# Sums of squares from the turned inputs, the order of two steps in the cross output, and where the mid tiles lie

## The reference, cut to what matters

```python
def rms_norm(x, g):
    y = x * lax.rsqrt(jnp.mean(x * x, axis=-1, keepdims=True) + RMS_EPS)
    return y * g

xn = rms_norm(h, norm_mix); proj = xn @ w_in               # h = x
# A: chunked attention, B: RWKV-7 time mixing, C: sliding-window attention, all read proj
h = h + concat([y_a, y_b, y_c]) @ w_out
xn = rms_norm(h, norm_x); mn = rms_norm(mem, norm_mem)      # cross attention, 4 heads of 128
q, k, v = xn @ x_wq, mn @ x_wk, mn @ x_wv
h = h + softmax(q k^T * 128**-0.5) v @ x_wo
h = h + relu(rms_norm(h, norm_mlp) @ mlp_w1)**2 @ mlp_w2   # width 8192
out = rms_norm(h, norm_final)
```

## Time and profile before

| | |
|---|---|
| median of 3 runs | 2789.34 us (2787.43 to 2789.41) |
| profiled execution, its own time | 2788.95 us |
| span of that execution, first to last instruction | 2787.2 us |
| TensorE matmul busy | 2723.8 us, 98% |
| VectorE busy | 1224.2 us, 44% |
| ScalarE busy | 803.2 us, 29% |
| GpSimd busy | 127.5 us, 5% |
| mean granted TensorE clock | 0.993 |
| DMA | 255.52 MB, mean 92 GB/s |

### The profile page before, as it was taken

How to read it: one execution, slowest core, us unless ns; L and a number is a source line. 1 busy time by engine, 2 the same in 40 slices (tenths; PEclk the granted TensorE clock), 3 DMA queues, 4 the chain that set the end, 5 groups by cost and what they waited for, 6 DMA issues and landing times.

```text
span 2787.2 us, 44304 instructions
## 1 busy us (share of the span) xinstructions
PE 2723.8 (98%) x18352; PEld 2158.9 (77%) x18352; DVE 1224.2 (44%) x1884; ACT 803.2 (29%) x1315; POOL 127.5 (5%) x240
## 2 busy tenths in 40 slices
PE   8999999999998999998899999999999999999997
PEld 6877777777777766886688888888888888888885
DVE  5266666666435545334433333333333333333333
ACT  4222222222124444344332221222212222122232
POOL 3000111001121110000000000000000000000000
PEclk9999999999999999999999999999999999999998
DMA  5321111111236522221133323322332223223322
GB/s 217 121 60 47 48 47 52 44 53 47 63 117 217 170 70 67 85 89 53 61 99 98 95 95 98 98 93 95 98 98 94 94 98 98 92 96 98 98 92 111
DMA packets 73148, 255.52 MB, mean 92 GB/s; under 512 B 8928, under 2 KB 9056, under 8 KB 71088
## 3 DMA queue, kind: packets, MB, share of 16 engines
q1 hardware_dynamic: 65664, 226.78, 25.4%
q0 software_dynamic: 7344, 26.69, 2.8%
HBM read 243.22 MB, written 10.22 MB: 91 GB/s over the span
## 4 chain that ended last, share of the span: by engine, by line
PE 95%; DVE 2%; DMA 1%; ACT 1%; issue 1%; DVEq 0%; POOL 0%; ACTq 0%; POOLq 0%
PE ps L1125 28%; PE ps L1126 26%; PE ps L1127 26%; PE ps L1144 9%; PE ps L1356 1%; PE ps L1335 1%; PE ps L1344 1%; DMA h<-in_mem_turned 1%; PE ps L1138 1%; DVE h L996 0%; DVE w_lo L710 0%; PE ps L1201 0%; PE ps L1198 0%; PE ps L1192 0%; PE ps L1181 0%
## 5 line engine op out<-in xcount | busy, mean ns | idle before, releaser
L710 DVE TENSOR_TENSOR w_lo<-w_raw,w_hi 128x1024 fp32r<-128x1024 f32 (+2 forms) x440 | 505.2, 1148 | 1163.0 <-ACT w_hi L434 1163.0
L434 ACT ACTIVATE w_hi<-w_raw 128x1024 fp32r<-128x1024 f32 (+2 forms) x440 | 438.9, 998 | 1566.0 <-PE ps L1127 1562.2
L1125 PE MATMUL ps<-act_hi,w_hi 128*128 128x512 f32 x1792 | 731.8, 408 | 14.9 <-DVE w_lo L710 11.5
L1127 PE MATMUL ps<-act_hi,w_lo 128*128 128x512 f32 x1792 | 701.6, 392 | 0.0
L1126 PE MATMUL ps<-act_lo,w_hi 128*128 128x512 f32 x1792 | 700.6, 391 | 0.0
L1125 PE MATMUL ps<-w_hi,mid_hi 128*128 128x512 f32 x1088 | 429.4, 395 | 8.1 <-DVE act_lo L752 6.7
L1126 PE MATMUL ps<-w_lo,mid_hi 128*128 128x512 f32 x1088 | 430.2, 395 | 0.0
L1127 PE MATMUL ps<-w_hi,mid_lo 128*128 128x512 f32 x1088 | 424.1, 390 | 0.0
L1125 PEld LDWEIGHTS ps<-act_hi,w_hi 128*128 128x128 f32 x1792 | 337.3, 188 | 108.0 <-DVE w_lo L710 12.0
L1127 PEld LDWEIGHTS ps<-act_hi,w_lo 128*128 128x128 f32 x1792 | 337.3, 188 | 73.0
L1126 PEld LDWEIGHTS ps<-act_lo,w_hi 128*128 128x128 f32 x1792 | 337.7, 188 | 68.7 <-issue 5.8
(11 more groups left out here) (273 smaller groups left out, 2404.7 us busy)
## 6 DMA issues: line engine op xcount, KB each, us to landing
w_raw<-in_w_rest SPq DMA_DIRECT2D x320, 512.0 KB, 3.4
w_raw<-in_w_pairs SPq DMA_DIRECT2D x112, 384.0 KB, 3.1
x_t<-in_x_turned SPq DMA_DIRECT2D x8, 512.0 KB, 8.7
x_mix<-in_x SPq DMA_DIRECT2D x4, 1024.0 KB, 13.3
qk<-scr_qkv POOLq DMA_DIRECT2D x16, 256.0 KB, 3.7
h<-in_x POOLq DMA_DIRECT2D x4, 1024.0 KB, 11.4
out<-h SPq DMA_DIRECT2D x4, 1024.0 KB, 4.3
scr_qkv<-pad POOLq DMA_DIRECT2D x15, 256.0 KB, 3.8
```

Of the source, the lines that this page charges most:

```text
L434: return nc.scalar.activation(dst, src, ACT.Copy, scale=scale)
L710: V.tensor_tensor(dst, w_raw[:, slot, 0:dst.shape[-1]], high.bitcast(F32), ALU.subtract).then_inc(s["w_split"], 1)
L1125: mm(dst, a_hi, b_hi, start=start, stop=False)
L1127: return mm(dst, a_lo, b_hi, start=False, stop=stop)
```

## The change

Five things are done.

1. x and mem are no longer loaded untransposed. ScalarE squares each turned tile (`squared`, into four buffers), VectorE adds the 16 squares up (`summed`), and one float32 ones matmul over the sum (`row_of_sums`) gives the sum of squares of every token on all partitions. Mean (`row_mean`, VectorE), root (`row_root`, ScalarE) and reciprocal (`inverse_row`, VectorE) are then done on the whole row, 512 or 256 wide. For x the squares stand in units 0 to 5 of g = 0, four tiles in each of units 0 and 1 and two in each of units 2 to 5. The matmul stands at p = 18, the start of unit 6. For mem they stand with the gained tiles at p = 13 to 20, and the matmul at p = 21 as before.
2. The values of the memory are scaled by the row where they leave PSUM, as the keys are; the later copy to `xv_tok` has no scale.
3. At the start the gain vector is loaded by SP as its first DMA. ScalarE and VectorE take tile 0, then the first weight unit, then tile 1; TensorE begins when tile 0 is there, and does all three outputs of tile 0 first.
4. In the cross output `turned_lo` stands ahead of `add_set`.
5. `rmem` goes and `rq` grows from 32 to 128 bytes, so everything behind it moves by 64 bytes: `h`, `mid_hi`, `mid_lo` and the RWKV tiles begin at 128 modulo 512.

```diff
-        rmem = sb("rmem", [P, 2])
-        rq = sb("rq", [P, 2, TT])
+        rq = sb("rq", [P, 8, TT])
...
-        x_mix = s1("x_mix", [P, TT, D])
+        x_sq = s1("x_sq", [P, 4, SEQ])
+        x_sum = s1("x_sum", [P, SEQ])
...
-        memx = h[:, 0:2, :]
+        mem_sq = h[:, 0, 0:4 * N_MEM].rearrange("p (i n) -> p i n", n=N_MEM)
+        mem_sum = h[:, 0, 4 * N_MEM:5 * N_MEM]
...  SP
+            sp.dma_start(gain[:, :, :], gains).then_inc(s["gain_in"], 16)
             for u in range(RAW):
                 turned_pair(u)
...
-                sp.dma_start(x_mix[:, u - RAW, :], x[(u - RAW) * P:(u - RAW + 1) * P, :]).then_inc(x_in[u - RAW], 16)
...  GpSimd
-            pool.dma_start(gain[:, :, :], gains).then_inc(s["gain_in"], 16)
+            step(nc.gpsimd.memset(ones[:, :], 1.0))
+            pool.sem_inc(s["ones_set"], 1)
...
-                    for t in range(2):
-                        pool.dma_start(memx[:, t, :], mem[t * P:(t + 1) * P, :]).then_inc(s["mem_in"], 16)
...  ScalarE
+            def squared(j, kt, dst, src):
+                if kt >= 4:
+                    act.wait_ge(s["sum_ready"], KT * j + kt - 3)
+                nc.scalar.activation(dst[:, kt % 4, :], src[:, kt, :], ACT.Square).then_inc(s["sq_ready"], 1)
+
+            def row_root(j, row, b, n):
+                act.wait_ge(s["row_mean"], j + 1)
+                nc.scalar.activation(row, row, ACT.Sqrt).then_inc(s["row_root"], 1)
...
                 if g == G_IN - 1 and p == 8:
-                    act.wait_ge(s["mem_in"], 32)
-                    for t in range(2):
-                        square_sum(t, 0, memx[:, t, 0:D // 2], mid_hi[:, 0:2, :].rearrange("p a b -> p (a b)"))
-                    root(1, 2)
                     act.wait_ge(s["memt_in"], 16)
                 for kt in mem_tiles(p, g):
+                    squared(1, kt, mem_sq, mem_t)
                     gained_hi(kt, 2, mem_hi, mem_t)
                 if g == G_IN - 1 and p == 23:
-                    act.wait_ge(s["row_mm"], 2)
-                    copy(mem_row, ps[:, 3, 0:N_MEM]).then_inc(s["row_ready"], 1)
+                    row_root(1, mem_row, 3, N_MEM)
...
-                    if g == 0 and u in (5, 6):
-                        for t in (2 * u - 10, 2 * u - 9):
-                            act.wait_ge(x_in[t], 16)
-                            square_sum(t, 0, x_mix[:, t, 0:D // 2], ps[:, 6:8, :].rearrange("p a b -> p (a b)"))
-                    if g == 0 and u == UNITS - 1:
-                        root(0, TT)
-                        act.wait_ge(s["consts"], 1)
-                        act.wait_ge(s["row_mm"], 1)
-                        copy(rms_row[:, :], bank(3)).then_inc(s["row_ready"], 1)
+                    if g == 0 and u < 6:
+                        for kt in (range(4 * u, 4 * u + 4) if u < 2 else range(2 * u + 4, 2 * u + 6)):
+                            squared(0, kt, x_sq, x_t)
+                    if g == 0 and u == 6:
+                        row_root(0, rms_row[:, :], 3, SEQ)
...
-                copy(xv_tok[:, kb, :], bank(6), scale=rmem[:, kb:kb + 1]).then_inc(s["xvt_ev"], 1)
+                copy(xv_tok[:, kb, :], bank(6)).then_inc(s["xvt_ev"], 1)
...  VectorE
+            def summed(j, kt, total, sq):
+                dve.wait_ge(s["sq_ready"], KT * j + kt + 1)
+                if kt == 0:
+                    V.tensor_copy(total, sq[:, 0, :]).then_inc(s["sum_ready"], 1)
+                else:
+                    dve.wait_ge(s["sum_ready"], KT * j + kt)
+                    V.tensor_tensor(total, total, sq[:, kt % 4, :], ALU.add).then_inc(s["sum_ready"], 1)
+
+            def row_mean(j, row, b, n):
+                dve.wait_ge(s["row_mm"], j + 1)
+                V.tensor_scalar(row, ps[:, b, 0:n], 1.0 / D, RMS_EPS, ALU.mult, ALU.add).then_inc(s["row_mean"], 1)
+
+            def inverse_row(j, row):
+                dve.wait_ge(s["row_root"], j + 1)
+                V.reciprocal(row, row).then_inc(s["row_ready"], 1)
...
                 for kt in mem_tiles(p, g):
+                    summed(1, kt, mem_sum, mem_sq)
                     gained_lo(1, kt, 2, mem_hi, mem_lo, mem_t)
+                if g == G_IN - 1 and p == 22:
+                    row_mean(1, mem_row, 3, N_MEM)
+                if g == G_IN - 1 and p == 23:
+                    inverse_row(1, mem_row)
...  VectorE, cross output
                 lo_next(G_XO, u)
+                if u % 2 and u > 1:
+                    turned_lo(3, u // 2 - 1, 3, tiles_of(act_hi), tiles_of(act_lo))
                 if u % 2:
                     add_set(UNITS * G_XO + u + 1, (S_XO + u // 2) % 2, u // 2)
-                if u % 2 and u > 1:
-                    turned_lo(3, u // 2 - 1, 3, tiles_of(act_hi), tiles_of(act_lo))
...  TensorE
+            def row_of_sums(j, total, n):
+                pe.wait_ge(s["ones_set"], 1)
+                pe.wait_ge(s["sum_ready"], KT * (j + 1))
+                mm(ps[:, 3, 0:n], ones[:, :], total, start=True, stop=True).then_inc(s["row_mm"], 1)
...
-                if g == 0 and p == 22:
-                    pe.wait_ge(s["diag_ready"], TT)
-                    row_of_roots(TT)
+                if g == 0 and p == 18:
+                    row_of_sums(0, x_sum[:, :], SEQ)
                 if g == G_IN - 1 and p == 21:
-                    pe.wait_ge(s["diag_ready"], TT + 2)
                     pe.wait_ge(s["var_eps"], PAIRS)
-                    row_of_roots(2)
+                    row_of_sums(1, mem_sum, N_MEM)
...
-                        pe.wait_ge(s["norm_lo"], 2 * u + 2)
+                        pe.wait_ge(s["norm_lo"], 2 * u + 2 if u else 1)
```

More of the change, by code:

```diff
@@ L484, in _ @@
             act.wait_ge(s["gain_in"], 16)
-            for n in range(SPL_IN - 1):
+            act.wait_ge(xt_in[0], 16)
+            gained_hi(0, 0, act_hi, x_t)
+            hi_in(0)
+            gained_hi(1, 0, act_hi, x_t)
+            for n in range(1, SPL_IN - 1):
                 x_hi(n)
@@ L756, in _ @@
             dve.wait_ge(s["zeroed"], 1)
-            for n in range(SPL_IN - 1):
+            dve.wait_ge(xt_in[0], 16)
+            gained_lo(0, 0, 0, act_hi, act_lo, x_t)
+            lo_in(0)
+            gained_lo(0, 1, 0, act_hi, act_lo, x_t)
+            for n in range(1, SPL_IN - 1):
                 x_lo(n)
@@ L911, in _ @@
                         lo_in(n)
[L912 to L918 removed]
+                    if g == 0 and u < 6:
+                        for kt in (range(4 * u, 4 * u + 4) if u < 2 else range(2 * u + 4, 2 * u + 6)):
+                            summed(0, kt, x_sum[:, :], x_sq)
+                    if g == 0 and u == 6:
+                        row_mean(0, rms_row[:, :], 3, SEQ)
+                        inverse_row(0, rms_row[:, :])
                     if g == 1 and u == 0:
                         dve.wait_ge(s["in_evac"], 3)
+                        dve.wait_ge(s["consts"], 1)
                         dve.wait_ge(s["lmu_in"], 16)
@@ L1003, in add_scaled_set, with scaled_by_row @@
                                            ALU.mult, ALU.add).then_inc(s["bank_evac"], 1)
+            def scaled_by_row(units, dst):
+                dve.wait_ge(s["w_used"], units)
+                dve.wait_ge(s["row_ready"], 2)
+                for m in range(4):
+                    V.tensor_tensor(dst[:, m, :], ps[:, m, 0:N_MEM], mem_row, ALU.mult).then_inc(s["bank_evac"], 1)
             def copy_set(units, sidx, dst, n):
@@ L1127, in split_mm @@
                 return mm(dst, a_lo, b_hi, start=False, stop=stop)
-            def row_of_roots(tiles):
-                pe.wait_ge(s["consts"], 1)
-                for t in range(tiles):
-                    last = mm(ps[:, 3, t * P:(t + 1) * P], ones[:, :], diag[:, t, :], start=True, stop=True)
-                last.then_inc(s["row_mm"], 1)
+            def row_of_sums(j, total, n):
+                pe.wait_ge(s["ones_set"], 1)
+                pe.wait_ge(s["sum_ready"], KT * (j + 1))
+                mm(ps[:, 3, 0:n], ones[:, :], total, start=True, stop=True).then_inc(s["row_mm"], 1)
             def turn_h(k, kt):
@@ L1303, in _ @@
                             kt = 2 * u + k
+                            if g == 0 and kt == 1:
+                                pe.wait_ge(s["norm_lo"], 2)
                             if kt == 0 and g:
```

49 lines of the change are left out of this document (12 added, 37 removed).

## The result

The changed kernel takes 2773.15 us (median of 4 runs, 2771.8 to 2775.31) beside 2789.38 us for the kernel before (4 runs, 2787.43 to 2791.83): ratio 0.9942, 95% interval [0.9925, 0.9959]. It is 16.2 us faster where 28 us were forecast, and 2773.15 lies outside the range of 2757 to 2769. The profiled execution took 2775.31 us, 2.2 above its median, so that its span is only 13.6 us shorter than that of before.

A forecast was written before the change was run, and what follows sets the result against it. TensorE, busy 2723.8 of 2787.2 us, was taken as the bound, leaving idle time and time per matmul. Terms -4.5 + 0.6 - 0.2 - 16.2 - 7.3 = -27.6 us on 2788.95 gave 2761.3 us, range 2757 to 2769.

The forecast's parts named there:

- the small products: Unit 7 of g = 0: eight small float32 matmuls, 2.08 us at the lower clock, replaced by one ones matmul of 1.0.
- Start and g = 0: Start to g = 1: TensorE starts at 7.35, waits 1.1 us for the sum in unit 6; -4.5 us, bounds -2.5 and -5.6.
- Mem row: g = 14: the 2.57 us wait goes, TensorE waits 2.9 for mem's sum; +0.6 us, bounds -0.5 and +3.5.
- the bound not taken: Mem row's upper bound: +3.5 us, with 0.42 us squares and adds and one more lower-clock stretch of 1.7.
- Cross output: Low halves ahead of the adds: three waits go, 10.5 us, and the slow stretches behind them, 5.7; -16.2 us.
- Where mid lies: Mid's tile from 64 to 128 modulo 512: 7.0 us as stationary operand, 0.3 moving; -7.3 us, bounds 0 and 7.6.
- the rival of another reason: Mid is slower for its role or how far up it lies, not its address: 2768.6 us; chance 0.13.
- The rule of the Trainium skill that the prediction weighed: Back-to-back 512-column matmuls 215.7 ns apart, no address term; by it mid's move is worth nothing, time 2768.6 us.
- VectorE being late in g = 0 and g = 14: Waits for the sums grow by 1.8 and 1.3 us, with 1.7 each of lower clock: 2767.8 us; chance 0.14.
- The cross output's wait staying: Cross output: the wait stays for something behind the same semaphore: 2777.5 us; chance 0.03.
- the small matmuls paying for the move: RWKV part: some 7,500 small matmuls each lose 6.6 ns by the 64-byte move, 50 us: 2811 us; chance 0.03.
- The rival on the slower side: The slower rival: RWKV's small matmuls pay for the 64-byte move, 2811 us; chance 0.03.

The follow-up runs named there:

- run 1: Changed kernel with 64 semaphore increments that nobody waits for at the start of TensorE's program: 2765.13 us, ratio 0.9908.
- run 5: Changed kernel with 8 increments at the start of TensorE's program: 2781.32 us in one run.
- run 9: Kernel before with one TensorE instruction fewer, a second wait for the same constants ahead of the row of mem: 2813.74 us, ratio 1.0099.
- run 2: Kernel before with 210 increments at the start of TensorE's program, which did not fit there: 2816.14 us, ratio 1.0085.
- run 3: Kernel before with one edit alone, the cross output's low halves ahead of the addition: 2772.99 us, ratio 0.9937.
- run 4: Changed kernel with the old layout, mid at 64 modulo 512 and all later tiles 64 bytes lower: 2778.97 us, ratio 0.9956.
- run 12: Changed kernel with the old order of the cross output and the old layout: 2797.09 us, ratio 1.0024.
- run 6: Changed kernel with 24 increments, mem's product at p = 23, and mem's views at 64 modulo 512 with mid at 128: 2761.32 us, ratio 0.9898.
- run 7: As run 6, but mid at 256 and the mem views at 192 modulo 512: 2779.32 us in one run.
- run 8: As run 6, but mid at 320 and the mem views at 256 modulo 512: 2767.57 us in one run.
- run 10: Changed kernel with 24 increments, mem's product at p = 23, weights and mid at 256 modulo 512, act at 128: 2787.53 us in one run.
- Run 11: As run 6, with 448 bytes behind mid so that the tiles behind it are at 64 modulo 512 again: 2761.40 us, ratio 0.9897.

## Why the prediction failed

**The step that failed is one that it does not have.** The sum has no term for where TensorE's loop lies among the blocks of its program. It costed the small products by their time alone (2.08 us for the eight of x), and put the 16 instructions that go, eight matmuls and eight weight loads, at nothing as instructions ahead of a loop. With 16 fewer the loop's body reaches over eight blocks instead of seven: 1598 instructions are six blocks and 62, so they fit into seven if the loop begins among the first 195 instructions of a block, and it went from the first back to the 241st. Here seven blocks stayed loaded through the turns (109 blocks in all), and with eight, nine were brought each time (163). The holes behind that cost 10.5 us in the trace of the changed kernel. That is 10.5 of the 13.9 us between the forecast's -27.6 and the measured -13.7; the mem row has 1.5 and the mem groups 1.3 of the rest. Runs 1, 5 and 9 moved the loop by increments or by one wait alone, and the holes went, moved and came. Run 1, where they are gone, has 2765.13 us, which lies in the range of the forecast; the 10.5 taken off 2773.15 would make 2762.6, against 2761 forecast. That all 10.5 come back in the medians is not shown: 8.0 did.

Why the hole's length changes is worked out, not measured. Hole and matmuls ahead of it make about the same sum: 2.5 to 3.1 us with none, 2.4 to 2.9 with three (0.7 us), 2.4 to 3.0 with six (1.4 us). With the end 46 instructions behind, some 20 matmuls or 4.6 us lie ahead (an estimate by 227 ns each), more than that sum, and no hole is listed.

The Trainium skill has the sizes, in "Runtime: NRT & Kernel Launch", section "Instruction fetch mechanics": TensorE's instruction memory holds 128 KiB and is refilled in blocks of 16 KiB, which are 256 instructions. An estimate from these figures is room for eight blocks, so that a loop over seven fits beside one fetched ahead and a loop over eight does not; the traces agree (0 and 9 blocks a turn). The same section of the Trainium skill also says that this memory is only two cache lines, and that a taken branch to a block outside the current window of two waits for its fetch. By that a loop over seven blocks would be fetched again in each turn; here none of it was, and the branch took 0.21 us, so for TensorE the measurement decides against it. It also says that crossing a block is mostly hidden. That agrees with run 2, whose window of w1 groups has 87.11 us against 87.04, and not with a block's end 1 to 16 instructions behind the turn, where the holes are 0.9 to 3.1 us.

**Start and g = 0**: right in mechanism, -4.1 for -4.5. The first matmul came at 7.81 and not 7.35, since tile 0 was begun at 5.38 and not 4.9 (the terms of the forecast add up to 7.26, not 7.35). From there to unit 6 TensorE took 27.4 us against 27.0 before, mostly because the lower clock at the start lasted 4.7 us of it and not 4.1. So unit 6 was reached at 35.2 and not 34.3. The sum was done at 35.7, later than the 35.4 forecast. The wait is 0.66 and not 1.1 only because TensorE came late to it, and the clock stayed at 1.00 behind it.

**Mem row**: the wait of 2.9 came as 3.18, and g = 15 follows unit 7's end by 2.94 where the forecast has 3.1. What was wrong is the bound not taken: behind the wait the granted clock was at its lower level from 855.58 to 858.99, so unit 7 ended 1.7 us later. The forecast had named that 1.7 as the upper bound, and +2.1 is inside its bounds. The clock did not fall each time: behind the same wait it fell in runs 4, 5 and 12 (3.0 to 3.4 us of waiting) and not in run 1 (2.92 us). The wait's length alone does not decide it: at g = 15 it fell in the kernel before at a wait of 2.67 us and stayed in run 4 at one of 2.93. Run 6 shows that the wait was avoidable: two places later the product finds its sum done, 3.9 us earlier at g = 15.

**Cross output**: right in mechanism and size. -16.6 over its stretch, and in run 3 by itself 17.4 us by the medians and 16.2 in the traces, idle time and half clock together; nothing took the wait's place.

**Where mid lies**: right in sign and size for the large part, 6.3 us of 6.6, and runs 4, 7, 8 and 10 show that it is the address, so the rival of another reason falls. The prediction read the address as a property of mid's tile. It is the distance to the other operand. The rule of the Trainium skill that the prediction weighed, with a fixed 2.5 ns and no term for an address (215.7 ns), is not what these rows show: the lowest mean over any window here was 226.7 ns. The forecast left the mem groups out, 384 matmuls whose moving operand is also mid. Their median went from 114 to 120 ns, 1.3 us the other way. Run 11 puts half of the median's change on the tiles behind mid; the other half, 117 against 120 with mem itself (and h) at 64 or 128, has the opposite sign from the 512 wide matmuls. Why is open.

**Rivals.** Of VectorE being late in g = 0 and g = 14 only the clock behind the mem wait came, 1.7 us; the waits were 0.66 for 1.1 and 3.18 for 2.9, not the 1.8 and 1.3 more of that rival. The cross output's wait staying and the small matmuls paying for the move did not come. The rival on the slower side was sought among prices of work. The one that came was a price of where code lies in the program, and the kernel before was one instruction away from it (run 9).

What else stays open: what decides whether the clock falls behind a wait of 3 us, why the profiled execution of the changed kernel took 2.2 us more than its median, and what in the hardware makes the operands' distance count.

## What to carry to other kernels

- An edit that changes how many instructions TensorE issues ahead of a long hardware loop moves the loop among the blocks of its code (other engines' loops were not tried). Compare the line of the instruction queue on the page before and after: if it grew by a multiple of the loop's turns, the loop no longer stays loaded. A few instructions ahead of it, where the engine is idle anyway, put it back. A releaser that has nothing to do with the waiting bank, at the same place in each turn, is the sign.
- Put the two operands of a matmul at the same address modulo 512, for fp32r matmuls of 512 columns: 2 to 7 ns of 227 on each, over thousands of them. The matmuls of 256 columns did not follow this.
- Three edits on top of the change (24 increments, mem's product two places later, the views of mem and h 64 bytes lower) give 2761.3 us, 0.9898 [0.9881, 0.9914] of the kernel before; of the order of two steps alone come 17 of these 28 us.

## What the runs showed of the hardware

- One instruction without effect, taken out of TensorE's stream, made a kernel 23.5 us slower (run 9); it stood in g = 14, some 700 us ahead of the loop that it moved.
- TensorE's sequencer ran 4.1 us ahead of its matmuls at the loop's turn; a branch of 3.9 us was hidden by that. The holes by the place of the block's end behind the loop's start: 1 instruction, 2.5 to 3.1 us; 8, 1.7 to 2.2; 16, 1.0 to 1.6; 46, 0.8 us in six turns together (run 9; run 5; the changed kernel, 0.9 to 1.3 in run 4; run 2).
- Matmuls of 512 columns in fp32r at the full clock were on average 226.7, 228.9, 232.4 or 233.3 ns apart, by the distance of their operands' addresses modulo 512.
- A semaphore increment on TensorE that nobody waits for took about 0.15 us at the start of its program: with 64 of them the first matmul came at 10.81 us (run 1), with 210 at 33.24 (run 2), 22.4 us for 146; with 24 it was not late at all (7.76, run 6).
